# Router logits in four column groups, normed rows kept by chunks, and a residual that ScalarE writes into PSUM

## The reference, cut to what matters

```python
def grouped_moe(h, router_w, router_bias, w_gate, w_up, w_down):
    xt = h.reshape(B * S, D)
    scores = jax.nn.sigmoid((xt @ router_w).astype(jnp.float32))
    biased = scores + router_bias
    ...                      # best of 4 groups, then the 2 best experts in it
    gate = ...               # (token, expert), zero where not chosen
    out = jnp.zeros_like(xt)
    for e in range(N_EXPERTS):
        he = jax.nn.silu(xt @ w_gate[e]) * (xt @ w_up[e])
        out = out + (he @ w_down[e]) * gate[:, e:e + 1]
    return out

for layer in range(DEPTH):
    ...                      # mix = the layer's attention
    x = layer_norm(DN_ALPHA * x + mix, ln_g[layer, 0], ln_b[layer, 0])
    ffn = grouped_moe(x, router_w, router_bias, w_gate[layer], w_up[layer], w_down[layer])
    x = layer_norm(DN_ALPHA * x + ffn, ln_g[layer, 1], ln_b[layer, 1])
```

## Time and profile before

| | |
|---|---|
| runs | 739.68, 739.78, 740.61 us, median 739.78 |
| profiled execution | 741.22 us, its span 739.4 us |
| TensorE busy | 721.2 us, 98% of the span |
| TensorE weight load busy | 391.8 us, 53% |
| VectorE, ScalarE, GpSimd busy | 281.5, 204.0, 110.1 us |
| mean granted clock of TensorE | 0.994 |
| moved by DMA | 245.06 MB, 331 GB/s over the span |

### The profile page before, as it was taken

How to read it: one execution, slowest core, us unless ns; L and a number is a source line. 1 busy time by engine, 2 the same in 40 slices (tenths; PEclk the granted TensorE clock), 3 DMA queues, 4 the chain that set the end, 5 groups by cost and what they waited for, 6 DMA issues and landing times.

```text
span 739.4 us, 9052 instructions
## 1 busy us (share of the span) xinstructions
PE 721.2 (98%) x3696; PEld 391.8 (53%) x3696; DVE 281.5 (38%) x528; ACT 204.0 (28%) x467; POOL 110.1 (15%) x91
## 2 busy tenths in 40 slices
PE   9999999999999999999999999999999999999994
PEld 5877766774344344343368886646434434434331
DVE  4485675363212121121257785526322212112114
ACT  4443689332101110110033555714111011011001
POOL 0011378322000000000052221401200000000001
PEclk9999999999999999999999999999999999999998
DMA  9999900167999999999999964017799999999992
GB/s 329 304 368 418 405 3 1 58 233 297 423 425 429 430 425 429 426 425 422 413 388 387 414 267 187 6 57 285 271 425 428 425 428 428 428 425 429 419 412 84
DMA packets 45596, 245.06 MB, mean 331 GB/s; under 512 B 6256, under 2 KB 10480, under 8 KB 31728
## 3 DMA queue, kind: packets, MB, share of 16 engines
q1 hardware_dynamic: 45552, 244.43, 82.0%
HBM read 243.37 MB, written 1.05 MB: 331 GB/s over the span
## 4 chain that ended last, share of the span: by engine, by line
PE 88%; DVE 6%; ACT 2%; POOL 1%; issue 1%; DMA 1%; SPq 0%; DVEq 0%; ACTq 0%
PE ps L963 30%; PE ps L986 15%; PE ps L883 5%; PE ps L996 4%; PE ps L630 4%; PE ps L632 3%; PE ps L631 3%; PE ps L948 3%; PE ps L776 2%; PE ps L762 2%; PE ps L801 2%; ACT R L1273 1%; PE ps L974 1%; PE ps L939 1%; DVE R L1591 1%
## 5 line engine op out<-in xcount | busy, mean ns | idle before, releaser
L963 PE MATMUL ps<-ring,R 128*64 128x512 f32 x928 | 226.7, 595 | 0.0
L963 PEld LDWEIGHTS ps<-ring,R 128*64 128x64 f32 x928 | 70.3, 137 | 108.8 <-issue 107.2
L986 PE MATMUL ps<-ring,R 128*64 128x512 f32 x448 | 113.4, 595 | 0.8 <-issue 0.8
L1224 ACT ACTIVATE wh<-ps,small 128x512 fp32r<-128x512 f32 x32 | 22.0, 687 | 262.3 <-PE ps L986 260.5
L986 PEld LDWEIGHTS ps<-ring,R 128*64 128x64 f32 x448 | 35.8, 137 | 67.1 <-issue 64.8
L1578 DVE TENSOR_TENSOR wl_r<-ring,wh 128x512 fp32r<-128x512 f32 x72 | 55.4, 787 | 39.7 <-ACT wh L1202 39.3
L1804 DVE SCALAR_TENSOR_TENSOR wl_r<-ps,small,wh 128x512 fp32r<-128x512 f32 x32 | 24.0, 751 | 105.5 <-ACT wh L1224 104.7
L630 PE MATMUL ps<-wh,xh_r 128*128 128x512 f32 x144 | 57.7, 400 | 1.1 <-DVE wl_r L1578 1.0
L1202 ACT CAST wh<-ring 128x512 fp32r<-128x512 f32 x72 | 44.5, 623 | 47.3 <-PE ps L632 45.3
L632 PE MATMUL ps<-wh,xl 128*128 128x512 f32 x144 | 56.3, 391 | 0.0
L631 PE MATMUL ps<-wl_r,xh_r 128*128 128x512 f32 x144 | 56.1, 390 | 0.0
(11 more groups left out here) (237 smaller groups left out, 998.4 us busy)
## 6 DMA issues: line engine op xcount, KB each, us to landing
ring<-in_w_gate SPq DMA_DIRECT2D x24, 2048.0 KB, 17.5
ring<-in_w_up SPq DMA_DIRECT2D x18, 2048.0 KB, 18.7
ring<-in_w_down SPq DMA_DIRECT2D x18, 2048.0 KB, 19.2
ring<-in_w_in SPq DMA_DIRECT2D x20, 1024.0 KB, 14.4
ring<-in_w_gate SPq DMA_DIRECT2D x16, 1024.0 KB, 15.5
ring<-in_w_down SPq DMA_DIRECT2D x24, 512.0 KB, 20.1
ring<-in_w_up SPq DMA_DIRECT2D x12, 1024.0 KB, 11.5
ring<-in_w_out SPq DMA_DIRECT2D x8, 1024.0 KB, 14.9
```

The source lines that it names most:

```text
L963: last = mm(ps[64 * e:64 * e + 64, to, :], xe[:, j, at + 64 * e:at + 64 * e + 64], slots[e][:, j * UNIT:(j + 1) * UNIT], start=(j == 0), s ...
L986: last = mm(ps[64 * e:64 * e + 64, 2 + w, :], hT[:, k, 64 * e:64 * e + 64], slots[e][:, at:at + UNIT], start=(k == 0), stop=(k == FJ - 1))
```

## The change

Seven edits that belong together:

1. The rows of X that the first norm writes are stored by chunks (`rows_at`, `ln_scale_chunks`, `ln_shift_chunks`): the norm's VectorE operations now read PSUM and the norm's weights with a stride of eight, and what reads X behind them reads runs.
2. `logits` uses the router's weights of two chunks as a 32-column stationary operand in four column groups and streams 128 tokens; ScalarE copies the 128x128 result (`logits_copy`), and `logits_folded` multiplies it with a 0/1 matrix that picks and adds the right sixteenths.
3. `seed` goes. ScalarE writes alpha * x into banks 4 to 7 (`seed_experts`); TensorE does nine short bfloat16 matmuls (`keep_warm`) where the eight float32 records were.
4. For pairs that gather, the transposes of the gate table stand behind those of the hidden rows, so that up follows gate directly.
5. The second gather stands ahead of down (into bank 0, behind the wait for VectorE's copy of the hidden transposes), so that the next gate follows down directly.
6. VectorE's slot tables and ScalarE's copy of gathered rows are put in the order that this needs.
7. `load_room` loads the first half of one chunk (number 11 of a layer, the second down of pair 1) into the space of the norm's weights as soon as the norm has read them, ahead of the loads that wait for the first gate.

```diff
+        ROOM = SLOT + 3
+        room = R5[:, 0:2 * D]
+        def chunks_at(what, j):
+            if what[0] == "moe" and what[1] % (6 * PAIRS) == ROOM and j < KJ // 2:
+                return room[:, j * UNIT:(j + 1) * UNIT]
+            return in_slot(what)[:, j * UNIT:(j + 1) * UNIT]
...
+            def load_room(n):
+                l = n // (6 * PAIRS)
+                sp.wait_ge(N.x_ready, ready(2 * l, T - 1, 1))
+                i, k = divmod(n % (6 * PAIRS), 6)
+                sp.dma_start(room, expert_src(l, 2 * i + k % 2, k // 2)[:, 0:2 * D]).then_inc(landing(("moe", n), 0)[0], 16)
...
                 for n in range(ahead, SLOT + 1):
                     load_expert(6 * PAIRS * l + n)
+                load_room(6 * PAIRS * l + ROOM)
                 load_quarters(6 * PAIRS * l + SLOT + 1)
...
-            def seed(bank, a, w, stop):
-                mm(ps[:, bank, :], const("alphai"), X[:, a, w * UNIT:(w + 1) * UNIT],
-                   start=True, stop=stop, skip_group_check=True)
...
-                for j in range(4 * w, 4 * w + 4):
-                    last = mm(ps[:, LOGITS[a], 0:E], yT[:, j, a * P:(a + 1) * P], grw[:, j, :],
-                              start=(j == 0), stop=(j == KJ - 1), skip_group_check=True)
+                for g in range(4):
+                    j = 4 * w + g
+                    two = grw[:, j - g % 2:j - g % 2 + 2, :].rearrange("p j e -> p (j e)")
+                    last = mm(ps[32 * g:32 * g + 32, LOGITS[a], P:2 * P], two, yT[:, j, a * P:(a + 1) * P],
+                              start=(w == 0), stop=(w == 1), skip_group_check=True)
+                if w:
+                    last.then_inc(R.xt, 1)
+            def logits_folded(l, a):
+                pe.wait_ge(R.xt_sb, rbase[l].xt_sb + 3 * a + 3)
+                last = mm(ps[:, LOGITS[a], 0:E], diag[:, :], const("fold"), start=True, stop=True, skip_group_check=True)
...
-                    last = mm(ps[:, bank, at * n:(at + 1) * n], rows[:, j, :],
+                    last = mm(ps[:, bank, at * n:(at + 1) * n], X[:, 1, j * P:(j + 1) * P],
...
+                    def gates_of_pair():
+                        pe.wait_ge(rd.gp, g + 1)
+                        if i:
+                            pe.wait_ge(rd.y_lo, 2 * n)
+                        transpose_gates(rd, 2 * (i % 2))
...
-                        if w and i % 2 and more:
-                            pe.wait_ge(rd.xa, 2 * g + 3)
+                        if i % 2 and more:
+                            pe.wait_ge((rd.xa, rd.xe)[w], 2 * g + 3)
+                        elif i and i % 2 == 0 and w == 0:
+                            pe.wait_ge(rd.xa, 2 * g + 2)
                         to_hidden(w, XeT[i // 2 % 2], P * (i % 2), slots[2 * w:2 * w + 2], done,
...
-                        if w == 0:
-                            pe.wait_ge(rd.gp, g + 1)
-                            if i:
-                                pe.wait_ge(rd.y_lo, 2 * n)
-                            transpose_gates(rd, 2 * (i % 2))
+                        if w == 0 and not more:
+                            gates_of_pair()
                     if i == 0:
                         pe.wait_ge(R.over, rbase[l].over + 1)
-                        seed(7, 1, 1, True)
+                        keep_warm(7, 1)
...
                     pe.wait_ge(rd.h, n + 1)
                     transpose_hidden(rd)
+                    if more:
+                        gates_of_pair()
...
                     pe.wait_ge(rd.ht_sb, n + 1)
+                    if more:
+                        gather(rd, 0, (2 * part + 2, 2 * part + 3), 4 * SLOTS)
                     pe.wait_ge(rd.gsum, n + 1)
...
-                    if more:
-                        pe.wait_ge(rd.xe, 2 * g + 2 + i % 2 + 1)
-                        gather(rd, 1, (2 * part + 2, 2 * part + 3), 4 * SLOTS)
...
-                mix_out(l, 1, 1, range(0, 4))
+                mix_out(l, 1, 1, range(0, 1))
+                logits_folded(l, 0)
+                mix_out(l, 1, 1, range(1, 4))
...
                 gather_tile(1, (2, 3), 4 * SLOTS, 0)
-                seed(4, 0, 0, True)
-                seed(5, 0, 1, True)
+                logits_folded(l, 1)
+                keep_warm(4, 3)
+                keep_warm(5, 3)
...
-                pe.wait_ge(N.x_ready, ready(2 * l, 1, 0))
-                seed(6, 1, 0, True)
+                keep_warm(6, 2)
                 experts(l)
...
+            def seed_experts(a, w):
+                nc.scalar.activation(ps[:, 4 + 2 * a + w, :].rearrange("p (c j) -> p j c", j=KJ), rows_at(a, w), ACT.Copy, scale=ALPHA
+                                     ).then_inc(seeded, 1)
...
+                def logits_copy(a):
+                    act.wait_ge(R.xt, C.xt + 3 * a + 3)
+                    copy(diag[:, :], ps[:, LOGITS[a], P:2 * P]).then_inc(R.xt_sb, 1)
...
+            def ln_scale_chunks(t, w):
+                c = slice(w * UNIT, (w + 1) * UNIT)
+                return stt(rows_at(t, w), by_chunk(ps[:, 2 * t + w, :]), mv[:, t, 0:1], by_chunk(lnw[:, 0, c]), ALU.subtract, ALU.mult)
+            def ln_shift_chunks(t, w):
+                c = slice(w * UNIT, (w + 1) * UNIT)
+                return stt(rows_at(t, w), rows_at(t, w), rstd[:, t:t + 1], by_chunk(lnw[:, 1, c]), ALU.mult, ALU.add)
...
-                    dve.wait_ge(rd.gt, n + 1)
-                    slot_tables(rd, i % 2)
+                    if not more:
+                        dve.wait_ge(rd.gt, n + 1)
+                        slot_tables(rd, i % 2)
...
                     copy_hidden(rd)
+                    if more:
+                        dve.wait_ge(rd.gt, n + 1)
+                        slot_tables(rd, i % 2)
```

More of the change, by code:

```diff
@@ L1 @@
 from collections import namedtuple
+from functools import partial
 from contextlib import ExitStack
@@ L41 @@
 _at = 0
-for _name, _n in (("ident", P), ("alphai", P), ("causal", P), ("before", P), ("ones", P),
+for _name, _n in (("ident", P), ("causal", P), ("before", P), ("ones", P),
                   ("cosq", T * DH), ("sinq", T * DH), ("cosk", T * DH), ("sink", T * DH),
-                  ("ccos", DH), ("csin", DH), ("slot", SLOTS), ("lower", EG * EG), ("valid", T), ("cmask", T * CS), ("side", P // CS)):
+                  ("ccos", DH), ("csin", DH), ("slot", SLOTS), ("lower", EG * EG), ("fold", E), ("valid", T), ("cmask", T * CS), ("side", P // CS)):
     CONST[_name] = (_at, _n)
@@ L84, in constants @@
     put("side", (p[:, None] // CS == np.arange(P // CS)[None, :]) * 1.0)
+    put("fold", (p[:, None] % 32 - 16 * (p[:, None] // 32 % 2) == np.arange(E)[None, :]) * 1.0)
     put("valid", tiles((np.arange(S) >= CL - 1)[:, None] * 1.0))
@@ L264, in build @@
         R = RT(*(sem(f"route_{n}") for n in RT._fields))
-        rbase = [RT(*[0] * len(RT._fields)), RT(scaled=1, stats=4, y_sb=4, grw=1, xt=4, xt_sb=4, logits=T, fixed=T, score=T, sel=T, pos=T, hot=1, table=1, over=1,
+        rbase = [RT(*[0] * len(RT._fields)), RT(scaled=1, stats=4, y_sb=4, grw=1, xt=6, xt_sb=6, logits=T, fixed=T, score=T, sel=T, pos=T, hot=1, table=1, over=1,
                                                xp=2 * T, xl=2 * T, ln_in=32)]
@@ L314, in in_slot @@
             return ring[:, n] if n < SLOT else extra
+        ROOM = SLOT + 3
[4 more added lines that the diff above has]
+            return in_slot(what)[:, j * UNIT:(j + 1) * UNIT]
+        spare_slots = [lambda j, n=n: ring[:, n, j * UNIT:(j + 1) * UNIT] for n in range(6)]
         def landing(what, h):
@@ L475, in load_half_freed @@
                             slot_free(what)
+                        if h == 0 and what[1] % (6 * PAIRS) == ROOM:
+                            continue
                         i, k = divmod(what[1] % (6 * PAIRS), 6)
@@ L1237, in experts @@
                     silu(rd)
+                    if i // 2 + 1 < DUOS:
+                        part = 2 * (i % 2) + 1
+                        act.wait_ge(rd.gathered, 4 * g + 4 + part + 1)
+                        copy_rows(rd, XeT[(i // 2 + 1) % 2], 0, range(2 * part, 2 * part + 2), 4 * SLOTS)
+                    if i == 0:
+                        seed_experts(1, 1)
                     act.wait_ge(rd.gsum, n + 1)
```

65 lines of the change are left out of this document (32 added, 33 removed).

## The result

The changed kernel took 750.59 us (median of 3 runs, 749.79 to 751.09), the kernel before 739.78: a ratio of 1.0133, 95% interval 1.0113 to 1.0152. It is 10.8 us slower, where 732.3 had been forecast. Its profiled execution took 750.59 (span 748.8), that of before 741.22 (span 739.4), so the two traces stand 9.4 us apart. The medians stand 10.8 apart because the profiled execution of before lay 1.4 above its median; its clock fell to 0.50 for 3.4 us in layer 1's routing.

What follows compares the result with a forecast made beforehand. TensorE was taken to bound the pairs, with DMA next. Pairs -7.2, layer 0's routing +0.4 and layer 1's -0.7 made -7.5 us, from a median of 739.78 to 732.3, range 730.0 to 736.8.

Steps and rivals of the forecast that it cites:

- The bound: Whole kernel: TensorE has 88% of the chain of waits and bounds the experts' pairs; DMA is next to be late.
- The pairs: Experts' pairs: fewer changes of matmul form gain 0.60 us a pair, 7.2 us over twelve, bounds 4.2 to 9.0.
- rival 3: Inside the pairs, between up and down: the clock falls, costing 1.5 us each time, up to 750.3 us; chance 0.05.
- DMA: Last up of a layer: slack of 1.7 us plus 2.5 from the early load, less the pairs' 3.6, leaves +0.6.
- Rival 1: Layers' ends: DMA becomes the bound, the pairs keep only 1.7 us in each layer, 736.1 us; chance 0.13.
- The routing: Logits, norm and gather of rows: edits 1 to 3 change layer 0 by +0.4 us and layer 1 by -0.7.
- Rival 2: Ahead of the experts: TensorE waits longer, the clock falls, 1.5 us lost in each layer, 735.3 us; chance 0.13.
- Both signs of the last paragraph: Signs of a wrong prediction: clock 0.5 beside the first gates, or TensorE standing still in the last pair.
- Layer 1's term of -1.3: Layer 1's routing, `fix_logits` to gather: TensorE's late queue, with the seeds in it, costs 1.3 us, which goes.
- The rival for the slower side: The same as rival 3: the clock falls inside the pairs, up to 750.3 us; chance 0.05.

Runs made afterwards that it cites:

- a5_old_pairs: a2 with the order inside the pairs as before (gate transposes behind gate, second gather behind down): 742.00 us, ratio 1.0021 to the kernel before.
- b4: The kernel before with the new order inside the pairs alone; routing, layout of the rows and loads as before: 738.94 us, ratio 0.9970.
- a3: a1 without the early load of the first half of chunk 11, which goes to its ring slot: 746.16 us, ratio 1.0072 to the kernel before.
- a1: The changed kernel without layer 1's jump to the next instruction block ahead of the last down product: 744.69 us, ratio 1.0061 to the kernel before.
- b3: The kernel before with 16 unused columns ending the table of constants, moving every tile behind it up by 64 bytes: 742.54 us, ratio 1.0021.
- b5: b4 with the first half of chunk 11 loaded early into a buffer of its own: 736.26 us, ratio 0.9926 to the kernel before.
- a6: a2 with the normed rows stored contiguously as before and the strides back in their readers: 738.75 us, ratio 0.9975 to the kernel before.
- b1: The kernel before with five one-column products (20 instructions) added in layer 1's routing, moving the jump behind a block boundary: 743.19 us, ratio 1.0032.
- after: The changed kernel with all seven edits, against the kernel before: 750.59 us, ratio 1.0133.
- a2: a1 with twelve more dummy products a layer in TensorE's two waits of the routing: 739.36 us, ratio 0.9976 to the kernel before.

## Why the prediction was wrong

**The bound.** This step was right for the kernel before: TensorE bounds all pairs there, and in a5_old_pairs too.

**The pairs.** The mechanism was right. The pair fell from 26.02 to 25.31 us, 0.71 instead of the forecast 0.60, just under the upper bound of 0.75; of that 0.63 belongs to the new order (b4) and the rest to the moved addresses. The covers held: the second gather follows the first without a wait. The clock did no harm inside the pairs, so rival 3 falls, as the window over five of them shows:

```profile
196.00:330.00 134.00, 134.00 (x668) 56.71 (x666) 25.40 (x39) 14.16 (x22) 3.14 (x3) 1.00 1.00 424
```

**DMA, the first step that failed.** The forecast had slack 1.7 + 2.5 - 3.6 = +0.6, called it nearly nothing, and took the pairs' gain whole. The slack measured 194.06 less 192.79 to 193.08 (b4), 1.0 to 1.3 us. The room gave 0.6 to 1.5 us (a3 against a1; 1.1 over all traces) and not 2.5. And the pairs wanted 6 x 0.71 = 4.3. That is -1.5 to -2.7, and in the changed kernel 4.3 - 2.36 = 1.9 us of each layer's gain is waited away. The sum was a difference near nought, and its sign had been trusted. Rival 1 had the outcome with 0.13, though not the cause: the room's load did land in idle time (issued at 168.19, landed 7.1 us later, with the DMA engines idle from 175 to 177.5), and half of what it gained was lost again later. Moreover the layer's end hangs on the first gate product, which releases the first slot: a microsecond lost in the routing isn't hidden by the later wait, but moves it.

**The routing, the second step that failed.** The failed step is that TensorE's idle time in the routing was counted at nothing. The seeds that the change took out were dismissed as work off the path, and with the shorter logits and the longer chain of VectorE that left waits of 1.54 and 1.29 us, behind which the clock fell to 0.50. Rival 2 had this with 0.13, but priced at 1.5 us a layer: measured are 6.35 - 3.72 = 2.6 in layer 0 and 6.64 - 3.72 = 2.9 in layer 1. Both signs of the last paragraph, clock 0.50 near the first gates and TensorE standing still in the last pair, came.

The other terms: VectorE's operations by chunks, forecast 1.074, measured 1.10 to 1.11. Tile 0's 16 records of the logits, forecast 0.9, measured 0.65. From `fix_logits` to the gather, forecast 5.7 to 5.8, measured 168.76 - 162.99 = 5.77 and 519.74 - 513.96 = 5.78. `gather_rows`, forecast 3.5, measured 3.72 at full clock. The gather's start in layer 0, forecast +1.0, measured +0.93: partly luck, as the projections' 5 ns had moved all of the routing by some 0.6 us.

Layer 1's term of -1.3 was wrong, though the interval fell by 0.5 as forecast. It had been read from one execution, in which the interval was 6.28 beside a clock of 0.50. In b3, b4 and b5, with the same routing at full clock, it is 4.99 (516.86 - 511.87 in b4), as in layer 0. So TensorE's late queue there came with the fallen clock and not from the seeds, and at full clock the change makes the interval 0.8 us longer in both layers. From the first logits to the gather's end it makes next to no difference (0.1 us), where +0.4 and -0.7 had been forecast.

**What was in no step.** The forecast for the profiled execution was 733.7 us and it took 750.59. The 16.9 us between them split by the instants of the first table. The layers' experts gained 4.7 instead of 7.2, which is 2.5 us. The stretches up to the first gates grew by 6.6 instead of falling by 0.3, which is 6.9: some 5 of it lies in the routing, where the clock was at half, and 1.9 in the tiles' addresses (0.6 in layer 0, 1.3 in layer 1). The end grew by 7.5, the wait at the jump (6.14 instead of 0.37) and the slower product behind it. Neither the jump nor the addresses were in any step or rival. Both follow from what the diff does without saying so: it adds instructions ahead of an alignment, and it changes the width of a table that stands ahead of other tiles. The rival for the slower side looked for one large cost inside the change's own mechanisms, where there was none; its time, 750.3, was hit for another reason.

**The gain that remains.** Of the seven edits, three carry it: the pairs' order (4 and 5) and the room (7), with 6 to serve them, 740.93 to 736.26 in b5. The logits in groups, the fold, the stored chunks and ScalarE's seeds bring nothing that could be measured.

## What to carry to other kernels

A slack that is the difference of three estimates is no slack: where a faster engine comes near the transfers' rate, work out both bounds and expect the later one, and look for what starts the transfers, since everything ahead of that moves the end. Before a product is taken off a tensor engine's queue, see what wait it filled and what the granted clock did there, and put dummies into the wait that the change leaves. Don't build a term on one execution whose clock row shows 0.50: look whether other executions of the same code show it. After any change in the count of instructions or in a tile's size, compare the untouched stages' mean durations and every idle time named "issue": in this case these showed the moved jump and the moved addresses.

## What the runs showed of the hardware

- With its jump to the next instruction block 2 or 3 slots behind a boundary, TensorE was idle for 4.97 and 6.14 us, and the product behind took 1.7 us more, at a clock of 0.50 to 0.63. With the jump 14 slots behind it the trace has 0.48 us of idle time, and ten runs lie from 0.2 to 4.5 us above the median of before.
- Products of 128x512 with `xh` or `xl` as the stationary operand took 400 and 390 ns with these tiles 128 bytes behind a multiple of 512, and 405 and 395 ns at 192 bytes: six kernels have the one, seven the other, without exception.
- VectorE's norm operations on 128x512 that read with a stride of eight float32 took 1.11 us (scale: PSUM and the weights strided) and 1.10 us (shift: only the weights), against 0.70 contiguous.
- Sixteen records of the logits took 1.85 us as 128x128 operands with 16 moving columns, and 0.65 us as 128x32 operands in four column groups with 128 moving columns, which take two more records (0.29 us) to fold.
- A layer's end followed its first gate product by 191.3 to 192.7 us in every kernel with new pairs and room, by 192.8 to 193.1 with new pairs alone, and by 193.8 to 194.2 with the old order.
- Near 90 us, in layer 0's attention, the clock fell to 0.50 for 3.4 or 6.8 us in seven of the thirteen traces (a1, a3, a6, b1, b3, b4, b5), with and without the change. From the first projection to the first logits a1 took 131.4 us with such a fall, where after and a2 took 130.0 and 130.1 without it. Single traces can differ by that much before any change acts.
